# A hybrid attention block on one core: two more pairs per sweep with seven products, their weight sums formed during attention

## The reference

```python
D_MODEL, SEQ = 2048, 256
D_FF = ((8 * D_MODEL // 3 + 255) // 256) * 256      # 5632
...
for l in range(DEPTH):
    h = rms_norm(x, ln1[l])
    p = h @ w_in[l]
    ...
    r_out = retention(rq, rk, rv, rg, ret_gn[l])
    s_out = swa_sink_attention(..., sinks[l])
    mix = jnp.concatenate([r_out, s_out.astype(r_out.dtype)], axis=-1)
    x = x + mix @ w_out[l]
    h = rms_norm(x, ln2[l])
    u = h @ w_ffn_in[l]
    a, b = jnp.split(u, 2, axis=-1)
    a = causal_depthwise_conv(a, conv_w[l], conv_b[l])
    x = x + (jax.nn.gelu(a, approximate=False) * b) @ w_ffn_out[l]
return rms_norm(x, ln_f)
```

## Time and profile before

| | us |
|---|---|
| runs before: median (lowest to highest of 3) | 1091.36 (1090.43 to 1093.61) |
| the profiled execution | 1090.57 |
| its span, first to last instruction | 1088.8 |
| PE busy | 1075.9 |
| DVE busy | 834.0 |
| ACT busy | 600.8 |
| POOL busy | 80.4 |

### The profile page before, as it was taken

How to read it: one execution, slowest core, us unless ns; L and a number is a source line. 1 busy time by engine, 2 the same in 40 slices (tenths; PEclk the granted TensorE clock), 3 DMA queues, 4 the chain that set the end, 5 groups by cost and what they waited for, 6 DMA issues and landing times.

```text
span 1088.8 us, 16760 instructions
## 1 busy us (share of the span) xinstructions
PE 1075.9 (99%) x5777; PEld 920.4 (85%) x5777; DVE 834.0 (77%) x1126; ACT 600.8 (55%) x806; POOL 80.4 (7%) x85
## 2 busy tenths in 40 slices
PE   8999999999999999999999999999999999999996
PEld 7888888888888888888888888888888888888885
DVE  6755777666668577968879678686788988898898
ACT  7445555555555454544545445455454777767773
POOL 2000111111100000101101011010010100000000
PEclk9999999999999999999999999999999999999999
DMA  9766555555599678797897887978877599869992
GB/s 346 263 190 194 159 170 157 157 171 166 164 325 351 177 267 311 225 337 253 281 324 230 317 269 253 351 213 320 283 238 276 178 315 323 305 231 311 328 334 81
DMA packets 163352, 276.06 MB, mean 254 GB/s; under 512 B 9091, under 2 KB 77537, under 8 KB 159984
## 3 DMA queue, kind: packets, MB, share of 16 engines
q1 hardware_dynamic: 162448, 273.39, 75.5%
q0 software_dynamic: 544, 1.69, 0.4%
q10 hardware_dynamic: 320, 0.47, 0.1%
HBM read 248.18 MB, written 27.26 MB: 253 GB/s over the span
## 4 chain that ended last, share of the span: by engine, by line
PE 97%; DVE 1%; DMA 0%; ACT 0%; issue 0%; DVEq 0%; ACTq 0%
PE acc L702 16%; PE acc L610 12%; PE acc L612 12%; PE acc L611 12%; PE acc L710 8%; PE bank_s L702 8%; PE bank_tr L702 8%; PE bank_tr L710 4%; PE bank_s L710 4%; PE bank_s L612 2%; PE bank_s L610 2%; PE bank_s L611 2%; PE bank_tr L612 1%; PE bank_tr L611 1%; PE bank_tr L610 1%; PE bank_s L758 0%
## 5 line engine op out<-in xcount | busy, mean ns | idle before, releaser
L973 ACT ACTIVATE w_hi<-raw 128x1024 fp32r<-128x1024 f32 x292 | 309.5, 1061 | 404.5 <-PE acc L612 135.7
L1259 DVE TENSOR_TENSOR w_lo<-raw,w_hi 128x1024 fp32r<-128x1024 f32 x292 | 356.1, 1224 | 186.5 <-ACT w_hi L973 185.6
L702 PE MATMUL acc<-h_both,w_hi 128*128 128x512 f32 x768 | 238.5, 392 | 0.0
L702 PEld LDWEIGHTS acc<-h_both,w_hi 128*128 128x128 f32 x768 | 137.9, 189 | 23.2 <-DVE rstd_row L1647 0.2
L710 PE MATMUL acc<-h_both,w_lo 128*128 128x256 f32 x768 | 154.2, 282 | 0.0
L710 PEld LDWEIGHTS acc<-h_both,w_lo 128*128 128x128 f32 x768 | 125.9, 191 | 7.5
L702 PE MATMUL bank_s<-h_both,w_hi 128*128 128x512 f32 x384 | 118.6, 390 | 0.0
L702 PE MATMUL bank_tr<-h_both,w_hi 128*128 128x512 f32 x384 | 118.6, 390 | 0.0
L610 PE MATMUL acc<-w_hi,h_both 128*128 128x512 f32 (+1 forms) x288 | 111.9, 389 | 1.0 <-DVE h_both L1273 1.0
L612 PE MATMUL acc<-w_hi,h_both 128*128 128x512 f32 (+1 forms) x288 | 109.0, 378 | 0.0
L611 PE MATMUL acc<-w_lo,h_both 128*128 128x512 f32 (+1 forms) x288 | 108.8, 378 | 0.0
(11 more groups left out here) (275 smaller groups left out, 1713.9 us busy)
## 6 DMA issues: line engine op xcount, KB each, us to landing
raw<-in_w_ffn_in SPq DMA_DIRECT2D x176, 512.0 KB, 4.3
raw<-in_w_in SPq DMA_DIRECT2D x130, 256.0 KB, 3.0
raw<-in_w_ffn_out SPq DMA_DIRECT2D x64, 512.0 KB, 6.2
stage<-in_w_ffn_out SPq DMA_DIRECT2D x24, 1024.0 KB, 8.3
kept_sums<-stage SPq DMA_DIRECT2D x24, 1024.0 KB, 6.5
raw<-kept_sums SPq DMA_DIRECT2D x24, 768.0 KB, 6.2
raw<-in_w_out SPq DMA_DIRECT2D x32, 512.0 KB, 4.9
raw<-in_w_in SPq DMA_DIRECT2D x19, 512.0 KB, 9.3
```

The lines of the kernel that those rows point to most:

```text
L702: ins = mm(banks[ft // 2][:, ft % 2, :], w_hi[:, slot, q * COLS + ft * P:q * COLS + (ft + 1) * P], h_both[:, 2 * k + q, :, :].rearrange("p ...
L973: run(w_hi[:, n % SPLIT, :], raw[:, n % RAW, :], ACT.Copy).then_inc(hi_ready, 1)
L1259: tt(w_lo[:, n % SPLIT, :], raw[:, n % RAW, :], w_hi[:, n % SPLIT, :].bitcast(F32), ALU.subtract).then_inc(lo_ready, 1)
```

## The change

Pairs 8 and 14 of each sweep become a `THIRD_SET`, and 14 of 22 pairs use seven products. The sums of weights for the four jobs (two sweeps by two pairs) are formed during attention in a buffer of their own, `head_stage` (buffer 4), which lies in memory that is given up after attention: SP issues the loads from the third head's tiles on and each store five tiles later, and VectorE does the subtractions behind `split(5)` and `split(6)` of attention steps 0 to 3. SP's loop over heads is written out, and VectorE's loop covers the first four steps only, the other four being written out. `token_sums` makes three sets instead of two, twelve instructions for eight. SP waits for the four stores ahead of the first staged load of the out projection, ACT and DVE wait for them with the others. The scratch for GpSimd's DMAs goes from 8192 to 4096 bytes.

```diff
 FIRST_SET = list(range(3, 19, 3))
 SECOND_SET = list(range(4, 20, 3))
+THIRD_SET = [8, 14]
+S_SETS = [FIRST_SET, SECOND_SET, THIRD_SET]
...
-S_SUMS = 8
-STAGE_USES = (11, 11, 1, 1)
+S_SUMS = 4 * len(S_SETS)
+HEAD_STAGED = [(sweep, p) for sweep in range(2) for p in THIRD_SET]
+HEAD_BUFFER = 4
+STAGE_USES = (11, 11, 1, 1, len(HEAD_STAGED))
...
+        head_stage = s1("head_stage", [P, 5, COLS])
...
+        def staging(j):
+            return head_stage[:] if j == HEAD_BUFFER else stage[:, j]
...
-            with sp.Fori(0, RET_HEADS // 2) as i:
-                for j in range(2):
-                    for k in range(8):
-                        n = HEAD_TILE + 8 * j + k
-                        load_head(i * 16 + n, n % RAW, i * 2 + j, k)
+            def head_traffic(n):
+                step, k = divmod(n - HEAD_TILE, 8)
+                store, fetch = step - 3, step - 2
+                if k == 3 and 0 <= store < len(HEAD_STAGED):
+                    stage_store(HEAD_BUFFER, 0, store, kept_index(*HEAD_STAGED[store]))
+                if k == 6 and 0 <= fetch < len(HEAD_STAGED):
+                    if fetch:
+                        sp.wait_ge(stage_stored[HEAD_BUFFER], 16 * fetch)
+                    sweep, p = HEAD_STAGED[fetch]
+                    stage_load(HEAD_BUFFER, sweep, 2 * p)
+
+            for n in range(HEAD_TILE, OUT_TILE):
+                load_head(n, n % RAW, (n - HEAD_TILE) // 8, (n - HEAD_TILE) % 8)
+                head_traffic(n)
...
                 if j == 0:
                     sp.wait_ge(mix_lo_ready, 2 * RET_HEADS)
+                    sp.wait_ge(stage_stored[HEAD_BUFFER], 16 * len(HEAD_STAGED))
...
+            def stage_sums(j, f, each, use, part):
+                b11, b12, b21, b22, fresh = (staging(j)[:, i, :] for i in range(5))
+                if part == 0:
+                    dve.wait_ge(stage_landed[j], f * (16 * each) + 16 * (use + 1))
+                    tt(fresh, b22, b12, ALU.subtract).then_inc(stage_summed[j], 1)
+                    tt(b12, b12, b11, ALU.subtract).then_inc(stage_summed[j], 1)
+                else:
+                    dve.wait_ge(stage_summed[j], f * (4 * each) + (4 * use + 2))
+                    tt(b22, b22, b12, ALU.subtract).then_inc(stage_summed[j], 1)
+                    dve.wait_ge(stage_summed[j], f * (4 * each) + (4 * use + 3))
+                    tt(b21, b21, b22, ALU.subtract).then_inc(stage_summed[j], 1)
...
-            with dve.Fori(0, RET_HEADS // 2 - 1) as i:
+            with dve.Fori(0, len(HEAD_STAGED) // 2) as i:
                 for j in range(2):
-                    attention_step(i * 2 + j, j, i + 4 * j, lambda k: lo(ahead + 8 * j + k, i, 16))
-            for s in (RET_HEADS - 2, RET_HEADS - 1):
+                    def split(k):
+                        lo(ahead + 8 * j + k, i, 16)
+                        if k in (5, 6):
+                            stage_sums(HEAD_BUFFER, i, 2, j, k - 5)
+                    attention_step(i * 2 + j, j, i + 4 * j, split)
+            for s in range(len(HEAD_STAGED), RET_HEADS):
                 attention_step(s, s % 2, s // 2 + 4 * (s % 2), lambda k: lo(ahead + 8 * s + k))
...
                     if last and 3 <= k < 7:
-                        token_sums(2 * (k - 3))
-                        token_sums(2 * (k - 3) + 1)
+                        for set_ in range(len(S_SETS)):
+                            token_sums(len(S_SETS) * (k - 3) + set_)
...
-    nc = bacc.Bacc("TRN2", target_bir_lowering=False, num_devices=1, dynamic_dma_scratch_size=8192)
+    nc = bacc.Bacc("TRN2", target_bir_lowering=False, num_devices=1, dynamic_dma_scratch_size=4096)
```

More of the change, by code:

```diff
@@ L81 @@
 SECOND_SET = list(range(4, 20, 3))
-SET = len(FIRST_SET)
-S_PAIRS = sorted(FIRST_SET + SECOND_SET)
-S_SLOT = {pair: i for i, pair in enumerate(FIRST_SET + SECOND_SET)}
-S_SUMS = 8
-STAGE_USES = (11, 11, 1, 1)
+THIRD_SET = [8, 14]
+S_SETS = [FIRST_SET, SECOND_SET, THIRD_SET]
+S_PAIRS = sorted(sum(S_SETS, []))
+S_SLOT = {pair: i for i, pair in enumerate(sum(S_SETS, []))}
+S_SUMS = 4 * len(S_SETS)
+HEAD_STAGED = [(sweep, p) for sweep in range(2) for p in THIRD_SET]
+HEAD_BUFFER = 4
+STAGE_USES = (11, 11, 1, 1, len(HEAD_STAGED))
 OUT_STAGED = [(0, 4), (1, 4), (0, 7), (1, 7)]
@@ L122, in kept_index @@
 def kept_index(sweep, p):
-    return 2 * SET * (p in SECOND_SET) + SET * sweep + (FIRST_SET if p in FIRST_SET else SECOND_SET).index(p)
+    own = [p in pairs for pairs in S_SETS].index(True)
+    return 2 * sum(map(len, S_SETS[:own])) + len(S_SETS[own]) * sweep + S_SETS[own].index(p)
 def raw_use(pair):
@@ L273, in build @@
         over_parts = ctx.enter_context(ExitStack())
-        stage = sb("stage", [P, len(STAGE_USES), 5, COLS], scope=over_parts)
+        stage = sb("stage", [P, HEAD_BUFFER, 5, COLS], scope=over_parts)
         over_parts.close()
@@ L512, in stage_load @@
             def stage_load(j, sweep, kt):
-                sp.dma_start(stage[:, j, 0:4, :].rearrange("p (k c) n -> p k (c n)", k=2),
+                sp.dma_start(staging(j)[:, 0:4, :].rearrange("p (k c) n -> p k (c n)", k=2),
                              w_ffn_out_v[:, bass.ds(kt, 2), 2 * sweep * COLS:2 * (sweep + 1) * COLS]
@@ L521, in stage_store @@
                 sp.dma_start(kept_sums[bass.ds(f + index, 1)].rearrange("o p n -> p (o n)"),
-                             stage[:, j, 1:5, :].rearrange("p c n -> p (c n)")).then_inc(stage_stored[j], 16)
+                             staging(j)[:, 1:5, :].rearrange("p c n -> p (c n)")).then_inc(stage_stored[j], 16)
             def load_half(half, x_sem, kv_sem):
@@ L1527, in turned_block @@
                     turned_lo(g, C_LN2, KT // 2 + g + 1)
[L1529 to L1542, removed]
             for n in range(OUT_TILE + 8, FFN_TILE):
@@ L1552, in _ @@
                 if 0 <= j < len(OUT_STAGED):
-                    stage_sums(j, 0, 0, part)
+                    stage_sums(j, 0, 1, 0, part)
             def sum_a(group, half):
@@ L1597, in token_sums @@
             def token_sums(k):
-                step, set_ = divmod(k, 2)
-                pairs = (FIRST_SET, SECOND_SET)[set_]
+                step, set_ = divmod(k, len(S_SETS))
+                pairs = S_SETS[set_]
                 gap = 2 * (pairs[1] - pairs[0])
@@ L1608, in token_sums @@
                     dve.wait_ge(g_ready, 2 * (GROUPS - 1))
-                    for j in (2, 3):
-                        dve.wait_ge(stage_stored[j], 16)
+                    for j in (2, 3, HEAD_BUFFER):
+                        dve.wait_ge(stage_stored[j], 16 * STAGE_USES[j])
                 else:
@@ L1627, in up_group @@
                     if last and 3 <= k < 7:
-                        token_sums(2 * (k - 3))
-                        token_sums(2 * (k - 3) + 1)
+                        for set_ in range(len(S_SETS)):
+                            token_sums(len(S_SETS) * (k - 3) + set_)
                     if not last and k >= 12:
-                        stage_sums((k - 12) // 2, turn, 2, k % 2)
+                        stage_sums((k - 12) // 2, turn, 1, 2, k % 2)
                     if last and k in (12, 13):
@@ L1655, in _ @@
                 if k >= 12:
-                    stage_sums((k - 12) // 2, 0, 1, k % 2)
+                    stage_sums((k - 12) // 2, 0, 1, 1, k % 2)
             with dve.Fori(0, GROUPS - 2) as f:
```

## The result

The changed kernel takes 1101.01 us (median of 6 runs, 1100.59 to 1103.07); the kernel before, in the same comparison, 1091.69 us (6 runs, 1090.43 to 1093.61). The ratio is 1.0087, with a 95% interval of 1.0077 to 1.0098: 9.3 us slower, where 1089.3 was forecast, and outside the range, which ended at 1093.2. The profiled execution took 1100.59 us.

What follows compares the result with a forecast made beforehand. TensorE was taken to bind, the DMA engines close behind in the last stage: 1090.57 us - 2.72 of matmuls + 0.7 of stall = 1088.55, with 0.79 for the median 1089.3 us; range 1087.5 to 1093.2.

Steps and rivals of the forecast that it cites:

- Matmuls: Last stage: four pairs go from 24 matmuls to 21, taking 4 x 0.68 = 2.72 us off the path.
- Attention: Attention steps 0 to 3: added loads, stores and VectorE's 2.5 us of subtractions hide in idle time, costing nothing.
- VectorE in the last stage, token sums: Last stage and last up group: VectorE's 4.95 us a seven and up to 2.7 us of third-set sums cost nothing.
- What the last stage must carry: Runs of five sevens: bytes at 360 GB/s against TensorE's time and lead; stall 0.7 us, bounds none and 3.2.
- its two terms, 0.3 and 0.5: Second sweep: TensorE waits 0.3 us at pair 39, then 0.5 us more by pair 41 through the output products.
- Rival 2: Last stage's four runs of five sevens: DMA engines become the bound, 6.2 us of stall at 316 GB/s, 1094.8 us; chance 0.15.
- Rivals 1 and 3: Last stage: no stall, 1088.6 us, chance 0.33. Attention: staged load late, 1.9 us in four steps, 1096.8 us, 0.05.
- The 1.25 us of lead in that bound: Last stage, 3.2 us stall bound: the run before (pairs 28 to 32) hands on a lead 1.25 us short.

Runs made afterwards that it cites:

- three_halves: Changed kernel with its seven-product pairs spread evenly (2, 3, 4, 6, 7, 8 to 18, 19) and rounding copy and subtraction done block by block: 1087.77 us.
- halves: Changed kernel with a pair's rounding copy and subtraction done block by block, each block's raw slot given back when that block is done: 1089.17 us.
- few_bytes: Changed kernel with the 768 KB load of sums of pairs 8 and 14 cut to 32 KB, seven products and four raw slots kept: 1100.14 us.
- slots_only: Changed kernel with pairs 8 and 14 back at eight products and two loaded pieces, but still holding four raw slots: 1097.39 us.
- halves_before: Kernel before the change, with a pair's rounding copy and subtraction done block by block: 1090.45 us.
- bytes_two: Changed kernel with pairs 8 and 14 back at eight products and two slots, plus three 256 KB loads beside each into two spare buffers: 1095.02 us.

## Why the prediction was wrong

- *Matmuls.* Right: 12 fewer, and 2.72 us where nothing else waits (2.65 to 2.68 in three_halves).
- *Attention.* Right in all its terms. The loads landed in 7.6 to 8.6 us (forecast: median 8.3), and the steps kept their length. The first subtraction took 1.24 us beside `mix_tok`, between the two values that the earlier trace rows gave. Two rows of after, `stage_load`'s landing and that subtraction:

```profile
DMA to landing us min/median/max: 7.6/7.9/8.6
```

```profile
112.87 1.24 DVE L1539 TENSOR_TENSOR head_stage<-head_stage 128x512 f32<-128x512 f32 x1
```

- *VectorE in the last stage, token sums.* Right: neither is in the way.
- *What the last stage must carry: the step that failed.* It put the stall at 0.7 us (its two terms, 0.3 and 0.5, make 0.8), bounds 0 and 3.2; the late starts are 12.4. It priced a run of five by bytes over a rate and let the lead absorb the rest, as if a load could always be issued in time. Why a load starts when it does was not asked. The rows to ask it were there: median landing 6.2 us and `w_lo` 2.29 us alone make 8.5 us, and the rounding copy ahead of `w_lo`, 1.9 us after, makes 10.4, before any issue or queueing; two sevens in a row leave 9.52, and the whole run with its eight 10.63. That shows a loop at its limit, not the loss: it takes the 12.4 to 14.0 us that a turn took after, and only the runs show those. The rate itself, taken as 360, was about right: halves shows 356 to 372.
- *Rival 2* named the place, four runs of five, both sweeps, and the sign, with 0.15. Its resource was wrong: the engines were not full. So was its price, 6.2 us of stall at 316 GB/s, since it let the rate limit the loop and not the loop the rate. It put the rate at which the change comes out even at 329 GB/s; its own formula gives 325.
- *Rivals 1 and 3*: no stall needs the shorter trip; no staged load came late.
- *Not in the sum at all*: the slower clock behind a wait, 1.6 us of the 12.4.

The range was too narrow for the reason that the step was wrong: its upper end was a stall from the same arithmetic. The 1.25 us of lead in that bound doesn't follow from the terms beside it either (2.9 lost and 2.5 regained leave 0.4).

## What to carry to other kernels

Where operands pass through a ring of buffers, price the trip as well as the bandwidth: release, issue, transfer, and each engine that works on the tile before its slot is free, against the time the consumer takes for as many slots as the ring has. A DMA share of 0.90 to 0.91 beside a waiting consumer did not mean full DMA engines here: with the loads issued earlier, the same bytes went at a share of 0.99. The cheap remedy was to work on a tile, and give its slots back, in smaller pieces, and to spread the tiles that hold many slots.

The Trainium skill, "Perfetto Trace Analysis", section Optimization Strategy, reads consistent bubbles on the engine that should be saturated as a hint that buffers are short; pairs 36, 37 and 38, late by 1.0, 2.0 and 0.6 us in a row, are such a case here.

## What the runs showed of the hardware

The granted clock fell to 0.50, which is 1.2 GHz, for 3.41 us behind a start of TensorE that was 2.0 us late and had one 1.0 us late 6.9 us ahead of it. A stretch of few_bytes, behind a start 3.0 us late, shows it again:

```profile
940.61:943.84 3.23, 3.23 (x9) 2.55 (x8) 3.23 (x4) 3.23 (x4) 0.00 (x0) 0.53 0.95 270
```

Not every such start is followed by a drop: one 2.3 us late in slots_only was not, nor were those 1.8 and 2.4 us late in few_bytes (1044.54 and 1056.91), nor, in the changed kernel, one 1.8 us late with one 0.7 us late 6.7 us ahead of it. It was seen in these profiles and not tried by itself.

halves_before is 1.3 us faster than the kernel before, whose profile has no late start in the last stage. Its runs lie within 0.5 us (1090.15 to 1090.61); those of the kernel before spread over 3.3 us (1090.44 to 1093.71). Some of them may lose a little in the same loop, which stands close to its limit there; no profile shows it, and it stays open.

Why 0.79 MB more beside each of four pairs costs 3.5 us in bytes_two, and why cutting as much saved next to nothing in few_bytes, the runs don't separate from the order in which the loads stand in the queue. That stays open too.
